# Routing of a mixture of experts: all choices compared in one step, the softmax behind the mask, the first gather ahead of the others, and biases in two rounded parts

## The reference, cut to what matters

```python
logits = (xt @ w_router + b_router)            # 512 x 32
top_vals, top_idx = lax.top_k(logits, 4)
top_gates = softmax(top_vals)                  # weights of the four choices
# each expert e on the rows that chose it, each row's result into its own place
gate = xb @ w_gate[e] + b_gate[e]
up = xb @ w_up[e] + b_up[e]
gate = minimum(gate, 7.0); up = clip(up, -7.0, 7.0)
y = (gate * sigmoid(1.702 * gate) * (up + 1.0)) @ w_down[e] + b_down[e]
# a token's output is the sum of its four results, weighted by top_gates
```

## Time and profile before

| | us |
|---|---|
| median of 3 runs | 1958.47 (1956.51 to 1958.64) |
| the profiled execution | 1957.12 |
| its span, first to last instruction | 1955.9 |
| TensorE busy in the span | 1851.6 (95%) |
| VectorE busy | 1403.7 (72%) |
| ScalarE busy | 1163.9 (60%) |
| GpSimd busy | 254.0 (13%) |

### The profile page before, as it was taken

How to read it: one execution, slowest core, us unless ns; L and a number is a source line. 1 busy time by engine, 2 the same in 40 slices (tenths; PEclk the granted TensorE clock), 3 DMA queues, 4 the chain that set the end, 5 groups by cost and what they waited for, 6 DMA issues and landing times.

```text
span 1955.9 us, 20832 instructions
## 1 busy us (share of the span) xinstructions
PE 1851.6 (95%) x8267; PEld 1456.2 (74%) x8267; DVE 1403.7 (72%) x1183; ACT 1163.9 (60%) x867; POOL 254.0 (13%) x201
## 2 busy tenths in 40 slices
PE   7999768999999999999999999999999998996998
PEld 5777647888888788888788888888856766675876
DVE  4466568999999899999899899898856122236342
ACT  4353346777777777777777777777733344443221
POOL 1311410211111111112112112111010011101000
PEclk9999779999999999999999999999979999997999
DMA  7321347999999999999999999999963321112201
GB/s 248 107 86 44 130 149 292 366 357 363 365 364 359 373 358 355 372 354 357 371 355 360 373 357 361 365 357 372 355 232 147 119 65 43 43 38 86 86 33 44
DMA packets 95043, 487.16 MB, mean 249 GB/s; under 512 B 13832, under 2 KB 15408, under 8 KB 44768
## 3 DMA queue, kind: packets, MB, share of 16 engines
q1 hardware_dynamic: 81120, 462.64, 63.7%
q0 software_dynamic: 9520, 17.13, 2.3%
q10 hardware_dynamic: 4304, 6.03, 1.0%
HBM read 481.56 MB, written 20.97 MB: 257 GB/s over the span
## 4 chain that ended last, share of the span: by engine, by line
PE 85%; DVE 6%; ACT 4%; DMA 1%; issue 1%; POOL 1%; ACTq 0%; SPq 0%; DVEq 0%; POOLq 0%
PE PS L431 78%; PE PS L663 3%; PE PS L844 2%; DVE WL L1210 2%; POOL Pp L1765 1%; PE PS L835 1%; DVE Pp L1573 1%; ACT WH L896 1%; ACT Pp L1143 1%; ACT Pp L1141 1%; ACT Pp L1139 1%; DMA ring<-in_w_in_dram 0%; PE PS L463 0%; DMA xg<-h2d,tok 0%; DMA yk<-yd 0%
## 5 line engine op out<-in xcount | busy, mean ns | idle before, releaser
L1210 DVE TENSOR_TENSOR WL<-ring,WH 128x2048 fp32r<-128x2048 f32 x428 | 972.1, 2296 | 293.2 <-ACT WH L896 293.1
L896 ACT ACTIVATE WH<-ring 128x2048 fp32r<-128x2048 f32 x428 | 816.2, 1915 | 390.6 <-PE PS L431 389.1
L431 PE MATMUL PS<-WH,xh 128*128 128x512 f32 x1024 | 332.6, 406 | 2.4 <-DVE xl L1449 2.4
L431 PE MATMUL PS<-WL,xh 128*128 128x512 f32 x1024 | 320.8, 394 | 0.0
L431 PE MATMUL PS<-WH,xl 128*128 128x512 f32 x1024 | 320.1, 394 | 0.0
L431 PEld LDWEIGHTS PS<-WL,xh 128*128 128x128 f32 x1024 | 193.2, 189 | 44.6
L431 PEld LDWEIGHTS PS<-WH,xl 128*128 128x128 f32 x1024 | 192.9, 188 | 44.6
L431 PEld LDWEIGHTS PS<-WH,xh 128*128 128x128 f32 x1024 | 189.4, 190 | 43.3 <-DVE xl L1449 2.8
L1734 POOL DMA_INDIRECT yd<-ys,dst x32 | 65.4, 2044 | 993.2 <-ACT ys L1054 993.2
L431 PE MATMUL PS<-WH,hh 128*128 128x512 f32 x512 | 163.5, 400 | 2.6 <-DVE hl L1449 2.6
L431 PE MATMUL PS<-WH,hl 128*128 128x512 f32 x512 | 160.4, 394 | 0.0
(11 more groups left out here) (341 smaller groups left out, 2247.6 us busy)
## 6 DMA issues: line engine op xcount, KB each, us to landing
ring<-in_w_gate_dram SPq DMA_DIRECT2D x128, 1024.0 KB, 7.2
ring<-in_w_up_dram SPq DMA_DIRECT2D x128, 1024.0 KB, 7.2
ring<-in_w_down_dram SPq DMA_DIRECT2D x128, 1024.0 KB, 8.3
ring<-in_w_in_dram SPq DMA_DIRECT2D x32, 1024.0 KB, 5.6
ring<-in_w_out_dram SPq DMA_DIRECT2D x8, 1024.0 KB, 5.0
yk<-yd SPq DMA_DIRECT2D x6, 1024.0 KB, 7.1
X<-in_x_dram SPq DMA_DIRECT2D x4, 512.0 KB, 9.9
h2d<-HV ACTq DMA_DIRECT2D x4, 512.0 KB, 3.1
```

Of the source, the lines that this page charges most:

```text
L431: return P.matmul(ps, a, b, start=start, stop=stop)
L896: A.activation(WH[buf[n]], ring[n % NR], ACT.Copy).then_inc(s_hi, 1)
L1210: V.tensor_tensor(WL[buf[n]], ring[n % NR], WH[buf[n]].bitcast(F32), SUB).then_inc(s_lo, 1)
```

## The change

- The biases are split into two parts rounded to float32r instead of three in bfloat16. ACT writes the first (a copy behind the last `h2T`), DVE the second (a subtraction ahead of `LG`). POOL's six instructions are gone. The matmul that adds them has 64 rows of float32r in place of 96 of bfloat16.
- `spread_out` works on all four choices at once: one comparison and one product of 128x512 elements and one sum over the innermost four. The comparison `eq` is made once and used for `DV` and for `Gt`.
- The division of the softmax moves behind the mask `M16`, and `M16` is made from `DV` straight away.
- POOL clears `xg` when the logits are there. The one-hots do not wait for it.
- The index step is done for expert 0 alone first, each expert's sum in a PSUM bank of its own (7, 4, 5); the gathers wait for their own index only. The count of experts with over 128 rows comes behind the index steps.
- Tiles of the routing lie elsewhere in SBUF.

The diff, cut to its core:

```diff
-    b3 = place("b3", [96, 2, D], BF16)
-    sel96 = place("sel96", [96, 32], BF16)
+    sel64 = place("sel64", [64, 32], F32R)
+    b3 = reg("b3", [64, 2, D], F32R, 44)
...
     def spread_out(o, v):
-        io = C[:, IOTA:IOTA + 32].unsqueeze(1).broadcast_to([128, 4, E])
-        for k in range(4):
...
+        V.tensor_tensor(e2, eq, v.unsqueeze(2).broadcast_to([128, 4, E, K]), MUL).then_inc(dv.sem, dv.one())
+        V.wait_ge(dv.sem, dv.n)
+        return V.tensor_reduce(o, e2, AX, ADD)
...
     def tensor_turn_rows(e):
-        P.wait_ge(s_ix, min(e + NI, E))
+        P.wait_ge(s_ix, min(e + NI, E) if e else 1)
...
     def tensor_gate_up(e):
-                    last = mm(PS[:, 2 * which + hf, :], sel96[:, e:e + 1].broadcast_to([96, 128]), b3[:, which, 512 * hf:512 * hf + 512], False, True)
+                    last = mm(PS[:, 2 * which + hf, :], sel64[:, e:e + 1].broadcast_to([64, 128]), b3[:, which, 512 * hf:512 * hf + 512], False, True)
...
         keep_h2(3)
+
+        A.wait_ge(s_bst, 48)
+        A.activation(b3[0:32], bst, ACT.Copy).then_inc(s_bh, 1)
         A.wait_ge(s_mxd, 1)
...
         low(first + NS - 1)
+        V.wait_ge(s_bh, 1)
+        V.tensor_tensor(b3[32:64], bst, b3[0:32].bitcast(F32), SUB).then_inc(s_b3, 1)
         V.wait_ge(s_lgt, 4)
...
         V.wait_ge(s_cnt, 1)
+        V.wait_ge(s_h2, 64)
+        vector_one_hot(0)
+        vector_index(0, 7)
+        for q in range(1, NI):
+            vector_one_hot(q)
+        for q in range(1, NI):
+            vector_index(q, (4, 5)[q - 1])
...
     def vector_experts():
-        V.wait_ge(s_mz, 2)
-        V.wait_ge(s_h2, 64)
-        for q in range(NI):
-            vector_one_hot(q)
-        vector_index(0, NI)
+        vector_further_count()
         low(first + NX - 1)
+        V.wait_ge(s_gk, 1)
         spread_out(Gt, GK).then_inc(s_sp, 1)
...
     def gpsimd_experts():
-        G.wait_ge(s_pos, 1)
-        G.wait_ge(s_b3, 1)
+        G.wait_ge(s_lgt, 4)
```

More of the change, by code:

```diff
@@ L86, in program @@
     B3 = at[0]
-    b3 = place("b3", [96, 2, D], BF16)
+    at[0] += 4 * KB
     bd = place("bd", [32, D], F32)
     GtT = place("GtT", [32, 4, 128], F32)
-    sel96 = place("sel96", [96, 32], BF16)
+    sel64 = place("sel64", [64, 32], F32R)
     FC = place("FC", [128, 40], F32)
-    st = place("st", [128, 64], F32)
+    st = place("st", [128, 32], F32)
     wgr = place("wgr", [128, 8, 8], F32)
@@ L165, in program, with routing @@
     tri16 = reg("tri16", [128, 2, 128], F16, 31.5)
[L166 to L179, removed]
+    HV = [reg(f"HV{i}", [128, D], F32, (40, 80.5, 56, 60)[i]) for i in range(4)]
+    row = [B3]
+    def routing(name, shape, dt):
+        size = (int(np.prod(shape[1:])) * 4 + 31) // 32 * 32
+        row[0] += size
+        return place(name, shape, dt, row[0] - size)
+    LG, DV, M, Gt = (routing(n, [128, 4, E], F32) for n in ("LG", "DV", "M", "Gt"))
+    M16 = routing("M16", [128, 4, E], F16)
+    mx, mf = (routing(n, [128, 4, 8], F32) for n in ("mx", "mf"))
+    mi = routing("mi", [128, 4, 8], U32)
+    nm, sm = (routing(n, [128, 4], F32) for n in ("nm", "sm"))
+    eq = reg("eq", [128, 4, E, K], F32, 22)
+    e2 = reg("e2", [128, 4, E, K], F32, 24)
+    b3 = reg("b3", [64, 2, D], F32R, 44)
     bst = reg("bst", [32, 2, D], F32, 64.25)
-    r1 = reg("r1", [32, 2, D], F32, 72.5)
     xg = [reg(f"xg{i}", [128, D], F32, 4 * i) for i in range(2)]
@@ L652, in tensor_routing, with tensor_index @@
         last.then_inc(s_pos, 1)
-    def tensor_index(q, column):
+    def tensor_index(q, bank):
         P.wait_ge(s_oh, q + 1)
         for j in range(4):
-            last = mm(PS[:, 7, column:column + 1], oh[q % NI][:, j], DV16[:, j, q:q + 1], j == 0, j == 3)
+            last = mm(PS[:, bank, 0:1], oh[q % NI][:, j], DV16[:, j, q:q + 1], j == 0, j == 3)
         last.then_inc(s_im, 1)
@@ L1245, in vector_mixer @@
         low(ahead(n_v))
-        for i in range(3):
-            V.tensor_copy(sel96[32 * i:32 * i + 32], C[0:32, IDENT:IDENT + 32])
+        for i in range(2):
+            V.tensor_copy(sel64[32 * i:32 * i + 32], C[0:32, IDENT:IDENT + 32])
         low(ahead(n_v + 1))
@@ L1409, in vector_routing @@
         V.tensor_copy(mf, mi).then_inc(dv.sem, dv.one())
+        V.wait_ge(dv.sem, dv.n)
+        V.tensor_tensor(eq, C[:, IOTA:IOTA + 32].unsqueeze(1).unsqueeze(3).broadcast_to([128, 4, E, K]),
+                        mf[:, :, 0:K].unsqueeze(2).broadcast_to([128, 4, E, K]), ALU.is_equal).then_inc(dv.sem, dv.one())
+        V.wait_ge(dv.sem, dv.n)
+        spread_out(DV, C[:, TOKK:TOKK + 16].rearrange("p (j k) -> p j k", j=4)).then_inc(dv.sem, dv.one())
+        V.wait_ge(dv.sem, dv.n)
+        V.tensor_scalar(M16, DV, 0.0, None, ALU.is_gt).then_inc(s_m16, 1)
+        V.tensor_scalar(M, DV, 0.0, None, ALU.is_gt)
+        V.tensor_copy(DV16, DV).then_inc(dv.sem, dv.one())
         V.wait_ge(s_ek, 1)
@@ L1413, in vector_routing @@
         V.tensor_tensor(GK, GK, sm.unsqueeze(2).broadcast_to([128, 4, 4]), MUL).then_inc(s_gk, 1)
-        spread_out(DV, C[:, TOKK:TOKK + 16].rearrange("p (j k) -> p j k", j=4)).then_inc(dv.sem, dv.one())
-        V.wait_ge(dv.sem, dv.n)
-        V.tensor_scalar(M, DV, 0.0, None, ALU.is_gt).then_inc(dv.sem, dv.one())
-        V.tensor_copy(DV16, DV)
-        V.wait_ge(dv.sem, dv.n)
-        V.tensor_copy(M16, M).then_inc(s_m16, 1)
         V.wait_ge(s_pos, 1)
```

62 lines of the change are left out of this document (20 added, 42 removed).

## The result

The changed kernel is slower by 0.28%: 1963.06 us, median of nine runs (1960.38 to 1966.51), against 1958.47 (1956.51 to 1960.05, nine runs as well), a ratio of 1.0028 with a 95% interval of 1.0018 to 1.0039. The forecast was 1947.0. Its profiled execution took 1960.5 us, with a span of 1959.1.

The account below looks back on a forecast made before the run. TensorE was taken to bound the expert part, so only an earlier start helps: 2.95 + 7.8 = 10.75 us, giving 1946.4 from the profiled execution or 1947.7 from the median, stated as 1947.0; likeliest 1944.6 to 1949.5, 8 in 10 1941.5 to 1952.0.

Parts of the forecast that it names:

- Part 1: Before the logits: with the biases off POOL, `HV[2]` is ready sooner and the turns start earlier, 2.95 us gained.
- the rival: TensorE's clock stays full through the turns and router matmuls: 7.3 us here instead of 2.95, total 1942.0; chance 14%.
- Part 2: Before `LG`: bias copy on ACT and subtraction on DVE cost 0, unless the clock stays full.
- a cover of 1.9 in the forecast: Before `LG`: DVE's bias subtraction ends at 236.6, 1.9 us before the logits at 238.5.
- Parts 3 to 6: From `LG` to expert 0's first matmul: mask 3.0, one-hot 1.55, first index 1.35, gather 1.9 us; 7.8 us taken together.
- The 7.4 us to landing: First gather, if the `low` were not what slowed it: up to 7.4 us to land, giving 1948.3.
- Part 7: The 128 bias matmuls in the expert part: 0 expected, bounds a slight gain and 11.5 us lost.
- The other-side rival: Expert part: both float32r bias loads of each pair exposed, 24.2 us added, 1970.6; chance 7% for exposure in part or whole.

Follow-up runs that it names:

- the bf16 one put back: Changed kernel with its 64 bias rows in bfloat16, tiles put 64 bytes higher again, where the changed kernel has them: 1959.61 us, ratio 1.0013.
- the kernel with 128 rows and moved: Changed kernel with the bias matmul on 128 float32r rows and all tiles behind the row picker 64 bytes lower: 1925.74 us, ratio 0.9827.
- the last experiment: Against the 128-row kernel with tiles 64 bytes lower, all twelve one-hots again ahead of the three index steps: 1926.13 us, ratio 0.9828.

## Where the prediction was right and where it failed

**Part 1** right in its mechanism. `HV[2]` takes 1.29 us without POOL's work, and 4.21 to 4.27 in the five kernels that have it. From `HV[0]` to `LG` the work costs 3.8 to 4.9 us where the clock falls to half, forecast 2.95, so the term was too small. In the changed kernel itself the clock held, and 7.6 us were gained; this is the rival, which had 7.3. It is not a property of the change: of the kernels with the same 2.24 us gap the bf16 one put back held too (PEclk 1.00 in 221.9 to 230.1), and the eleven others fell to half clock, with 6.87 us for the 32 router matmuls. Each kernel has one trace; of the nine executions of the changed one the two fastest, one of them the profiled, had a mean granted clock of 0.982, the others 0.978 to 0.980, so it may not have held in all of them.

**Part 2** right as conditioned. With the clock held the cover was gone, and `LG` at 231.40 came right behind the subtraction (229.09 + 2.28). In the kernel with 128 rows and moved it came from the matmuls, with DVE idle for 1.97 us, against a cover of 1.9 in the forecast:

```profile
237.65 0.29 DVE L1397 TENSOR_TENSOR LG<-PS,brc 128x128 f32<-128x128 f32 x1 [1.97 <-PE PS L424]
```

**Parts 3 to 6** right. Behind `LG`, in the changed kernel: `eq` 0.69 us long (forecast 0.71), `P1` at 4.88 (4.95), first one-hot at 5.31 (5.4), the gather at 7.97 (8.0), landed 4.33 after its issue (4.3), `xl` at 15.64 (16.55), first matmul at 16.91 (17.85). The gather was waited for by the turn (3.62 us) and then hidden behind DVE, which ends last, as said. The 0.9 us that it is better come from DVE: in the order written, the two `low` and `Gt` end at 247.1, 15.7 behind `LG`, earlier than I had stacked them.

POOL's part of the first gather took 1.15 us with no `low` beside it; in the last experiment the second gather took 2.31 while two `low` ran, as 2.26 before, and the third 0.99 with DVE idle. The traces say more: in the changed kernel 29 gathers were issued while a `low` ran, and each of these POOL instructions ended 0.86 to 0.89 us after the end of that `low`, with 2.25 to 2.95 us in all. The one that was issued 0.34 us before a `low` took 1.00. So POOL's part stands still until the running `low`, a `tensor_tensor` with both inputs in SBUF, has ended. The Trainium skill ("SBUF — State Buffer", Who interferes with whom) has a `tensor_tensor` leave such descriptors alone, an inference by its own words. The rows show it held up, and they decide. The 7.4 us to landing that I had worked out under that rule did not come about, but how much of the old 7.4 to 8.4 us was this wait isn't isolated by any run.

**Part 7** is the step that failed, and it alone turned the sign. It said that a bias matmul costs nothing new, since a load lies beside the matmul ahead wherever TensorE has no gap, and it bounded a surprise at 11.5 us. It was 25.7, and the sign that the prediction had named itself, that the expert part grows, came true. Four things were wrong. The load of 64 rows was priced by rows of 128 and of 96, none of 64, and the row count was not looked at as a size of its own: I called the matmuls the same because the columns were the same. The overlap was taken for granted, against the row that it cites: the earlier trace rows has 15.8 us of idle time ahead of the 96-row loads, and they began with their own matmul and not beside the one ahead. With 64 rows four loads in a row come late, those of the two bias matmuls and of the two behind them, each by about 0.1 us. The bound counted only the 0.09 by which two loads differ, twice in each place. And a busy share of 100% was read as proof that nothing can be hidden in the stretch, though a busy row takes in a slower one. The other-side rival was right that the load might not run ahead, and had the size (24.2), but by another sum: it took both loads of a pair as exposed in full, and laid that to the type and the repeated column, which cost next to nothing with 96 and 128 rows. It stood at 7%.

The total for parts 1 to 6 was forecast at 10.75 us, 1947.0. The kernels in which only the rows are mended take 1947.94 and 1947.12. This is a close hit, but not a clean one: with 128 rows, where the clock fell as forecast, the first matmul of expert 0 comes 13.35 us earlier, 2.6 more than forecast, while the expert part is 3.3 longer than before. That the two nearly cancel is luck. Of the 3.3 us the bias places explain 1.0; the rest isn't settled, and the large tiles lie 64 bytes from those of the kernel before.

**The rest of the span** behind the expert part is 6.0 us shorter in the changed kernel. Before and after, by windows of 20 us in the stage that follows (same columns as the windows above):

```profile
1420.00:1440.00 20.00, 17.40 (x73) 14.06 (x72) 8.24 (x5) 5.12 (x4) 1.32 (x1) 0.91 0.43 152
1440.00:1460.00 20.00, 18.22 (x27) 7.25 (x26) 12.41 (x8) 7.91 (x6) 3.03 (x3) 0.59 0.70 273
```

```profile
1420.00:1440.00 20.00, 17.60 (x79) 13.84 (x78) 17.00 (x10) 10.85 (x7) 0.98 (x1) 1.00 0.80 287
1440.00:1460.00 20.00, 18.63 (x54) 10.52 (x52) 6.33 (x3) 7.91 (x6) 3.02 (x3) 0.84 0.31 107
```

Part of it is the clock, 0.91 and 0.59 before, 1.00 and 0.84 after, though the stage doesn't lie at quite the same time in both. Over all kernels this rest took 524 to 531 us with no order that I could tie to an edit. No step of the forecast spoke of it.

## What to carry to other kernels

Price an inserted matmul by a row with its own row count as well as its columns and its type, and if no such row exists, say so and bound it by the distance of starts, not by the load; here padding 64 rows with zeros to 96 or 128 was worth 15 us (1963.06 to 1947.94) for work that changes nothing. Where an engine is busy for the whole of a stretch, compare the number of instructions in two equal windows, since the busy share can't show that they have become slower. Look at PEld too: idle time ahead of its load, where the other loads have none, was the sign here. And before small gains are compared, hold the addresses of the large tiles fixed: here 64 bytes were worth 13 to 22 us, and all parts of the change together 10.5 (1958.47 to 1947.94, with 128 rows).

## What the runs showed of the hardware that I had not expected

- A pair of 64-row matmuls between 128-row ones costs 0.27 to 0.28 us over the same pair with 96 rows in bf16 (three kernels), and 0.38 to 0.40 over 96 or 128 rows in float32r (two); with 96 or 128 rows float32r costs 0.02 more than 96 rows of bf16. The pair that follows is longer too, 0.73 us against 0.62 with 128 rows. The weight load of 64 rows begins 0.32 us after the start of the 128-row matmul ahead, in either type, and that of 96 or 128 rows of float32r 0.003 us after it. Why it is so at 64 and not at 96 is not shown; sizes other than 64, 96 and 128 weren't run.
- Float32r products of 512 columns follow each other at 0.227 to 0.233 us by where their operands lie in SBUF, 3%, at the full clock and with the same neighbours; 64 bytes decide. The token rows matter most, and a buffer of weights moved alone can do harm.
- Behind the turn's wait of 2.24 us, and with the same narrow matmuls, TensorE stayed at 2.4 GHz in two kernels and fell to 1.2 GHz in the eleven others with the same wait (3.66 against 6.87 us for the 32 router matmuls); what tips it is not shown. It was worth 2.8 to 4.2 us at this point, 25.6 against 28.3 to 29.7 us from `HV[0]` to `LG`.
- POOL's instruction of an indirect gather takes 1.0 us alone and, issued while a `tensor_tensor` of 2048 elements runs on DVE, ends 0.86 us or a little more after that one's end (29 gathers of the changed kernel).
